# A hybrid decoder layer in five blocks: the edges between its stages rearranged, its up products cut into wider groups

## The chip, the cores and the metric

The kernel runs on one core of a Trainium2 chip. The metric is the device time of one execution in microseconds (us), median of three runs. The engines, as the profile names them: PE (TensorE, matmuls; PEld is its weight load), DVE (VectorE), ACT (ScalarE), POOL (GpSimd), SP (SyncE, which here only issues DMAs). Each engine runs its own instructions in order, and semaphores order them between engines. SBUF is the on-chip memory, PSUM the banks into which PE sums; DMAs move data between these and HBM.

## The reference

One decoder layer over 2048 prompt rows of 1024 columns and 8 x 4 sample rows. Norms are RMS norms; a conditioning vector gives a scale, a shift and a gate for each half of the layer.

```
mod  = silu(c) @ w_ada + b_ada                   # six vectors of 1024
h    = rmsnorm(x, g_pre_mix) * (1 + scale) + shift
p    = h @ w_in                                  # q, k, v, z, beta/decay; attention q, k, v
q, k, v = silu(causal conv, 4 taps)              # group A: gated DeltaNet, 4 heads x 128, chunked
oA   = gated delta rule(q, k, v, beta, g, state) # its state is an output, so is the conv's last rows
oB   = sliding window attention, window 128, with sinks   # group B: 8 query, 2 key heads x 64
x1   = x + gate * rmsnorm(concat(oA, oB) @ w_o, g_post_mix)
h2   = rmsnorm(x1, g_pre_ffn) * (1 + scale) + shift
y    = x1 + gate * rmsnorm(square(relu(h2 @ w_up)) @ w_down, g_post_ffn)   # 4096 hidden columns
```

Outputs are y for prompt and samples and the updated states and caches.

## The kernel before

All matrices are multiplied in three passes (`three_pass`, L79 to L84): both factors are split into a high and a low part of a reduced format, and hi x hi, hi x lo and lo x hi are summed in PSUM. ACT makes a high part by a casting copy, DVE the low part by subtracting it from the raw values. The layer is five blocks, one behind the other; at the end of each, its semaphores are cleared behind a barrier of all engines (`clear_sems`, L73), and the next block begins.

- `prologue` (L86): conditioning, the first four groups of w_ada (`group`, L286; `turn_rows` turns their rows into columns), small vectors turned into columns (L318 to L321), norm and turn of the first four x tiles and the samples (`square`, `norm`, `turn`, `evac`). SP issues every load; PE's turn of the vectors waits for all fifteen small loads, the last of which are the attention sinks (L139).
- `projection` (L339): h stays in SBUF, transposed, in four blocks of 512 rows plus 4 leading and 8 sample columns; w_in comes in 22 chunks of 128 columns for each block, 88 in all. For a chunk SP loads w_in (double buffered), ACT and DVE split it (`split`), PE sums two groups of 262 columns (48 matmuls), ACT evacuates (L568), and DVE and ACT run the four taps and silu (12 "conv" chunks of a block), silu alone, or a plain copy into `so`. POOL keeps the samples' columns and stores `so` to HBM (L793, through its software DMA queue); two zero stores (L778) begin its list. In the first three blocks, four x tiles each for the next block are squared, normed (`norm`, L700) and turned by PE (L463) between chunks: twelve in all.
- `mixer` (L1319): delta rule and attention tile by tile (16 tiles), an order written out by hand. POOL stores the outputs of a tile (L2178, L2182); at the end it waits for the last of them, issues four stores of states (L2207 to L2211), and waits for these.
- `out_projection` (L2228): tile by tile, 48 matmuls of 512 columns. At the start ACT and DVE split w_o (eight slices), PE spreads two gate rows (`spread_gate`, L2216), ACT evacuates them, and then the first tile's casts follow. `pre` is the product of a tile, `post` norm, gate and residual.
- `mlp` (L2499): two halves of the rows (`Half`, L2467; 1056 with the samples, 1024). Over pairs of hidden chunks, `up` makes 128 hidden columns at a time for all rows of the half, in four groups of 264 or 256 (one PSUM bank each), ACT relu, DVE square and split; `down` adds two hidden chunks' products to y for each tile of 128 rows (L2778). At a half's last `down`, each tile runs: add, mean square (ACT, DVE), pow -0.5 on POOL (L2737), scale and gate on DVE (`scale_out`, L2791), addition of x1 on POOL (`residual`, L2727), store by SP (L2603). POOL's order is pow of tile t, residual of tile t-1. SP loads x1 for tile t once tile t-2 is done. The second half's w_up and first up products stand behind or beside this.

Of the kernel before, what the change touches and what calls it, by code (L numbers as in the profile page):

```python
# [85 lines left out]
def prologue(nc, io, k):  # L86

    with ExitStack() as ctx:
# [17 lines left out]
        s_vec, s_c = m.sem("vectors_loaded"), m.sem("c_loaded")  # L106
# [9 lines left out]
        n_vec = 8 + 3 + NS  # L116
# [3 lines left out]
        with nc.Block() as block:  # L120
            @block.sync
            def _(sp):
                flat = lambda v: v.rearrange("a (c p) -> (a c) p", p=P)
                sp.dma_start(cin[0:1, :], io["c_prompt"]).then_inc(s_c, 16)
# [6 lines left out]
                for g in range(GA):  # L131
                    sp.dma_start(wa[:, g], io["w_ada"][:, g * 512:(g + 1) * 512].rearrange("(k p) n -> p k n", p=P)).then_inc(s_wa[g], 16)
                for t in ORDER:
                    src = io["xs"] if t == 4 else io["x"][t * P:(t + 1) * P, :]
                    sp.dma_start(xt[0:rows(t), t], src).then_inc(s_x[t], 16)
                for src, dst in ((io["a_log"], k["alog"]), (io["dt_bias"], k["dtb"]), (io["sinks"], k["sink"])):
                    sp.dma_start(dst[:], src.partition_broadcast(P).rearrange("p a h -> p (a h)")).then_inc(s_vec, 16)
                for s in range(NS):
                    sp.dma_start(k["sink_s"][s * 4:s * 4 + 4, :], io["sinks"].rearrange("a (g c) -> (a c) g", g=2), allow_slow_non_contiguous=True  # L139
                                 ).then_inc(s_vec, 16)  # L140
                sp.wait_ge(s_vec, 16 * n_vec)
# [41 lines left out]
            def _(act):  # L183
# [20 lines left out]
                square(0)  # L204
                square(1)
                for i in range(5):
                    if i + 2 < 5:
                        square(i + 2)
                    evac(i)

            @block.vector
            def _(dve):
# [11 lines left out]
                dve.wait_ge(s_tr, 2)  # L224
                v.tensor_copy(k["vcol"][:], pc[:, 0, 0:NV]).then_inc(s_der, 1)
                v.tensor_scalar(k["taps"][:], pc[:, 0, 96:96 + CW * CC], 0.5, None, ALU.mult).then_inc(s_der, 1)
                v.tensor_copy(k["xs_pad"][:, :, :, 0:CW - 1],
# [111 lines left out]
def projection(nc, io, k):  # L339
# [6 lines left out]
    with ExitStack() as ctx:  # L346
# [51 lines left out]
        with nc.Block() as block:  # L398
            @block.sync
            def _(sp):  # L400
# [25 lines left out]
                for b in range(NBLK):  # L426
                    for c in range(NCH):
                        n = b * NCH + c
                        if n + 2 < NBLK * NCH:
                            load(n + 2)  # L430
# [2453 lines left out]
```

## Time and profile before

| what | us |
|---|---|
| median of 3 runs (lowest, highest) | 2997.35 (2995.22, 2998.13) |
| the profiled execution | 2993.79 |
| its span | 2992.0 |
| PE busy / DVE / ACT / POOL | 2718.8 / 1475.2 / 866.8 / 293.5 |
| up products, L81 to L83, 2048 each line (the page's group means overlap) | 580.0 + 582.9 + 580.2 |
| DVE's adds of down products, L2778, 272 | 331.9 |
| POOL's chunk stores L793, 88 | 3.6 median to landing |

Times count from the start of the span. PE's matmuls are pipelined, so that the mean duration of one (283 ns for an up product) is longer than its spacing, and spacing is taken from stretches without gaps. "Idle before" is the time that an engine stood still before an instruction, with what released it. Lines of DMA issues (SPq, and on POOL) show the engine's issuing time, not the transfer; "to landing" runs from issue to the end of the transfer. Clearing and barriers at a block's end are no busy time and show as idle before the next block's first instructions, released by "PEq L76" or "POOLq L76".

### The profile page before, as it was taken

To read this page: it belongs to the slowest core of one execution; us is meant where nothing else is said; L and a number is where in the kernel's file an instruction comes from. 1 tells how busy PE (TensorE), PEld (TensorE's weight loads), DVE (VectorE), ACT (ScalarE), POOL (GpSimd) and SP (SyncE) were. 2 spreads that over 40 slices of the span, in tenths; PEclk is the share of its full clock that TensorE was granted. 3 is DMA by queue.
4 is the path that set the end of the run, shared out by engine and by line. 5 is a ranking of instruction groups with operands and counts; after the bars stand their busy time and mean duration, and the time that the engine had idled before them with its cause. 6 is when DMAs were issued, how large, how long until landed. Compare 5 with 4: busy or idle time off the path is not lost. (4 is left out here: it accounts for less than half of the span.)

```text
span 2992.0 us, 45904 instructions
## 1 busy us (share of the span) xinstructions
PE 2718.8 (91%) x18524; PEld 2390.3 (80%) x18524; DVE 1475.2 (49%) x2020; ACT 866.8 (29%) x1634; POOL 293.5 (10%) x417
## 2 busy tenths in 40 slices
PE   4999999996487896998799999999989999999996
PEld 2898999994265664886789989898968998998994
DVE  3646464636567774454444444434454434434434
ACT  2434343323054454332312112121222221221221
POOL 1111111111011111111000000000032000000004
PEclk7999999997698998999999999999999999999998
DMA  6554545345384455454311101010143111111113
GB/s 227 154 163 133 174 124 180 116 135 169 86 237 123 131 155 144 141 171 130 113 52 33 56 28 56 28 56 28 57 152 96 38 56 46 38 56 46 38 57 112
DMA packets 354361, 309.38 MB, mean 103 GB/s; under 512 B 41964, under 2 KB 308499, under 8 KB 354220
## 3 DMA queue, kind: packets, MB, share of 16 engines
q1 hardware_dynamic: 341196, 263.85, 30.2%
q0 software_dynamic: 13040, 43.81, 4.2%
q8 instruction: 86, 1.41, 0.2%
q14 instruction: 39, 0.32, 0.0%
HBM read 235.85 MB, written 72.70 MB: 103 GB/s over the span
## 5 line engine op out<-in xcount | busy, mean ns | idle before, releaser
L81 PE MATMUL up_ps<-h_hi,w_up_hi 128*128 128x264 f32 (+1 forms) x2048 | 580.0, 283 | 21.8 <-DVE h_lo L2756 15.6
L82 PE MATMUL up_ps<-h_lo,w_up_hi 128*128 128x264 f32 (+1 forms) x2048 | 582.9, 285 | 0.0
L83 PE MATMUL up_ps<-h_hi,w_up_lo 128*128 128x264 f32 (+1 forms) x2048 | 580.2, 283 | 0.0
L2778 DVE TENSOR_TENSOR y<-y,down_ps 128x1024 f32<-128x1024 f32 (+1 forms) x272 | 331.9, 1220 | 318.2 <-PE down_ps L83 317.7
L81 PE MATMUL down_ps<-w_down_hi,u_hi 128*128 128x512 f32 x1088 | 434.8, 400 | 18.4 <-issue 9.9
L83 PE MATMUL down_ps<-w_down_hi,u_lo 128*128 128x512 f32 x1088 | 430.4, 396 | 0.0
L82 PE MATMUL down_ps<-w_down_lo,u_hi 128*128 128x512 f32 x1088 | 428.5, 394 | 0.0
L81 PE MATMUL proj_ps<-h_hi,w_in_hi 128*128 128x262 f32 x1408 | 407.0, 289 | 14.8 <-DVE h_lo L656 11.6
L81 PEld LDWEIGHTS up_ps<-h_hi,w_up_hi 128*128 128x128 f32 x2048 | 388.9, 190 | 24.5 <-issue 16.9
L82 PE MATMUL proj_ps<-h_lo,w_in_hi 128*128 128x262 f32 x1408 | 402.1, 286 | 0.0
L83 PE MATMUL proj_ps<-h_hi,w_in_lo 128*128 128x262 f32 x1408 | 401.5, 285 | 0.0
L82 PEld LDWEIGHTS up_ps<-h_lo,w_up_hi 128*128 128x128 f32 x2048 | 388.2, 190 | 1.3
L83 PEld LDWEIGHTS up_ps<-h_hi,w_up_lo 128*128 128x128 f32 x2048 | 386.6, 189 | 0.0
L2768 DVE TENSOR_TENSOR relu<-relu 128x1056 f32<-128x1056 f32 (+1 forms) x64 | 81.6, 1274 | 492.3 <-ACT relu L2696 492.3
L81 PEld LDWEIGHTS proj_ps<-h_hi,w_in_hi 128*128 128x128 f32 x1408 | 267.8, 190 | 25.0 <-issue 24.6
L82 PEld LDWEIGHTS proj_ps<-h_lo,w_in_hi 128*128 128x128 f32 x1408 | 269.1, 191 | 0.0
L83 PEld LDWEIGHTS proj_ps<-h_hi,w_in_lo 128*128 128x128 f32 x1408 | 268.2, 190 | 0.0
L81 PEld LDWEIGHTS down_ps<-w_down_hi,u_hi 128*128 128x128 f32 x1088 | 206.1, 189 | 71.3 <-DVE y L2778 16.5
L83 PEld LDWEIGHTS down_ps<-w_down_hi,u_lo 128*128 128x128 f32 x1088 | 206.1, 189 | 48.5
L82 PEld LDWEIGHTS down_ps<-w_down_lo,u_hi 128*128 128x128 f32 x1088 | 207.2, 190 | 44.2
L2696 ACT ACTIVATE relu<-up_ps 128x264 f32<-128x264 f32 (+1 forms) x256 | 98.6, 388 | 486.3 <-PE up_ps L83 484.9
L2706 ACT CAST w_down_hi<-w_down_raw 128x1024 fp32r<-128x1024 f32 x64 | 64.0, 1049 | 603.4 <-PE down_ps L83 603.4
(494 smaller groups left out, 3667.4 us busy)
## 6 DMA issues: line engine op xcount, KB each, us to landing
w_in_raw<-in_w_in SPq DMA_DIRECT2D x88, 512.0 KB
w_up_raw<-in_w_up SPq DMA_DIRECT2D x66, 512.0 KB
w_down_raw<-in_w_down SPq DMA_DIRECT2D x64, 512.0 KB, 4.4
proj_scratch<-chunk_out POOLq DMA_DIRECT2D x88, 256.0 KB, 3.6
w_ada_cols<-in_w_ada SPq DMA_DIRECT2D x8, 2048.0 KB, 9.2
qkv<-proj_scratch SPq DMA_DIRECT2D x16, 768.0 KB, 6.8
p_w_ada_cols<-in_w_ada SPq DMA_DIRECT2D x4, 2048.0 KB, 15.3
prep_qk<-proj_scratch SPq DMA_DIRECT2D x16, 512.0 KB, 4.6
```

The costliest lines, as they stand in the source:

```text
L81: nc.tensor.matmul(out, whi, mhi, start=first, stop=False)
L82: nc.tensor.matmul(out, whi, mlo, start=False, stop=False)
L83: return nc.tensor.matmul(out, wlo, mhi, start=False, stop=last)
L2696: a.activation(ru[:, c, at], pu[:, j, 0:qn], ACT.Relu).then_inc(H.s_re, 1)
L2706: a.copy(dwh[:, c], dr[:, c]).then_inc(H.s_dwh, 1)
L2768: v.tensor_tensor(ru[:, c, 0:H.n], ru[:, c, 0:H.n], ru[:, c, 0:H.n], ALU.mult).then_inc(H.s_u, 1)
L2778: v.tensor_tensor(acc, acc, pd[r, (par * H.tiles + t) % 2], ALU.add).then_inc(H.s_y, 1)
```

## The change

In the order of the blocks. Prologue: loads in another order; the vectors' turn waits for eight loads, the other seven have a semaphore of their own; the norms and turns of x tiles lie between the groups; chunks 0 and 1 of w_in are loaded and split here. Projection: zero stores and chunk stores are issued by ACT; the store of chunk n-1 stands between the wait for chunk n's matmuls and chunk n's evacuation; one more `clear_sems` follows the block. Mixer: two state stores before the last tile's, two right behind the loop; their landing is waited for at the end of POOL's list in the out projection. Out projection: tile 0's casts before w_o's split, the first product waits slice by slice, the sample gate's spreading behind it. MLP: the second w_up load behind the h2 slices, h2 casts before its split and before the gate copies; groups of 352 columns (three) and 512 (two) instead of four; the residuals of odd tiles and of a half's last two tiles on DVE behind `scale_out`, with the semaphore of done tiles split by parity. The diff, cut:

```diff
                 sp.dma_start(cin[0:1, :], io["c_prompt"]).then_inc(s_c, 16)
                 sp.dma_start(cin[1:1 + NB, :], io["c_sample"]).then_inc(s_c, 16)
+                load_x(4)
+                load_ada(0)
+                load_x(0)
+                load_ada(1)
...
+                load_x(1)
+                load_ada(2)
+                load_x(2)
+                load_ada(3)
+                load_x(3)
+                for q in range(2):
+                    sp.dma_start(k["w_in_raw"][:, q], io["w_in"][:, q * P:(q + 1) * P].rearrange("(k p) n -> p k n", p=P)
+                                 ).then_inc(k["w_in_loaded"][q], 16)
...
+                                 ).then_inc(s_late, 16)
+                sp.wait_ge(s_late, 16 * (3 + NS))
...
-                square(0)
-                square(1)
-                for i in range(5):
-                    if i + 2 < 5:
-                        square(i + 2)
+                def split(n):
+                    act.wait_ge(k["w_in_loaded"][n], 16)
+                    a.copy(k["w_in_hi"][:, n], k["w_in_raw"][:, n]).then_inc(k["w_in_hi_split"], 1)
+
+                for i in range(4):
+                    square(i)
                     evac(i)
+                square(4)
+                split(0)
+                evac(4)
+                split(1)
...
+                norm(0)
                 rows_out(0)
+                norm(1)
                 rows_out(1)
+                dve.wait_ge(s_tr, 2)
...
                 columns(0)
+                norm(2)
+                columns(1)
                 rows_out(2)
-                columns(1)
-                norm(0)
-                norm(1)
+                norm(3)
+                columns(2)
                 rows_out(3)
-                columns(2)
-                norm(2)
+                norm(4)
                 columns(3)
...
+                turn(0)
                 group(0)
+                turn(1)
+                group(1)
                 pe.wait_ge(s_vec, 16 * n_vec)
...
                 last.then_inc(s_tr, 1)
-                group(1)
                 pe.wait_ge(s_der, 4)
                 turn_rows(0)
+                turn(2)
+                turn_rows(1)
                 group(2)
-                turn_rows(1)
+                turn(3)
+                turn_rows(2)
                 group(3)
-                turn_rows(2)
-                turn(0)
-                turn(1)
+                turn(4)
                 turn_rows(3)
...
-                load(0)
-                load(1)
+                load(2)
...
-                    if n >= 2:
-                        act.wait_ge(s_so, n - 1)
+                    if n > 0:
+                        store(n - 1)
                         act.wait_ge(s_keep, n - 1)
...
+                def store(n):
+                    c, at = n % NCH, n // NCH * BLK + PAD
+                    act.wait_ge(s_so, n + 1)
+                    act.dma_start(io["projT"][c:c + 1, :, at:at + BLK].rearrange("c p t -> (c p) t"), so[:, n % 2]).then_inc(s_st[n % 2], 16)
...
-                split(0)
-                split(1)
+                for q in range(2):
+                    act.dma_start(io["projT"][q * 11:q * 11 + 11, :, 0:PAD].rearrange("c p t -> p c t"),
+                                   k["zeros"][:].broadcast_to([P, 11, P])).then_inc(s_st[q], 16)
...
+                store(NBLK * NCH - 1)
+                for q in range(2):
+                    act.wait_ge(s_st[q], NBLK * NCH // 2 * 16 + 16)
...
-                    pool.wait_ge(s_so, n + 1)
-                    pool.dma_start(io["projT"][c:c + 1, :, b * BLK + PAD:(b + 1) * BLK + PAD].rearrange("c p t -> (c p) t"),
-                                   so[:, q]).then_inc(s_st[q], 16)
...
+                        if t == NT - 1:
+                            pool.wait_ge(s_st, NT)
+                            pool.dma_start(io["ssm_prompt"].rearrange("a b h k v -> k (a b h) v"), k["state"][:]).then_inc(s_fin, 16)
+                            pool.dma_start(io["swa_v_prompt"].rearrange("a b w g d -> (a b w) (g d)"), vt[:, 1, :]).then_inc(s_fin, 16)
...
-                pool.wait_ge(s_obst, 16 * NT)
-                pool.wait_ge(s_ost, 16 * NT)
-
-                pool.wait_ge(s_st, NT)
-                pool.dma_start(io["ssm_prompt"].rearrange("a b h k v -> k (a b h) v"), k["state"][:]).then_inc(s_fin, 16)
-                pool.dma_start(io["swa_v_prompt"].rearrange("a b w g d -> (a b w) (g d)"), vt[:, 1, :]).then_inc(s_fin, 16)
                 pool.wait_ge(s_fin0, 6)
                 pool.dma_start(io["swa_k_prompt"].rearrange("a b w g d -> (a b w) (g d)"), kl[:]).then_inc(s_fin, 16)
                 pool.dma_start(io["conv_prompt"].rearrange("a b i (c p) -> (a b i c) p", p=P), k["xrow"][:]).then_inc(s_fin, 16)
-                pool.wait_ge(s_fin, 64)
+                pool.wait_ge(s_obst, 16 * NT)
+                pool.wait_ge(s_ost, 16 * NT)
...
-                spread_gate(nc, pe, k, 0, TS, 0, True, pt[:, 1]).then_inc(s_gt, 1)

                 def pre(t, p, u):
-                    if isinstance(t, int) and t == 0:
-                        pe.wait_ge(s_wl, KD)
-                        pe.wait_ge(s_gr, 2)
                     pe.wait_ge(s_oh, t + 3)
                     pe.wait_ge(s_ol, t + 3)
                     pe.wait_ge(s_t, t + 1)
                     for kk in range(KD):
+                        if isinstance(t, int) and t == 0:
+                            pe.wait_ge(s_wl, kk + 1)
                         for h in range(2):
                             at = slice(h * 512, (h + 1) * 512)
                             last = three_pass(nc, po[:, p, h, :], ohi[:, p, kk, :], olo[:, p, kk, :],
                                               whi[:, kk, at], wlo[:, kk, at], kk == 0, kk == KD - 1)
                     last.then_inc(s_mm, 1)
+                    if isinstance(t, int) and t == 0:
+                        spread_gate(nc, pe, k, 0, TS, 0, True, pt[:, 1]).then_inc(s_gt, 1)

                 def post(t, p, u):
                     n = rows(t)
+                    pe.wait_ge(s_gr, 2)
...
+                act.wait_ge(s_w, 2 * KD * 16)
+                for c in range(KD):
+                    a.copy(whi[:, c], wr[:, c]).then_inc(s_wh, 1)
                 pre(1, 1, 0)
+                act.wait_ge(s_gt, 1)
+                a.copy(gate[:], pt[:, 0]).then_inc(s_gr, 1)
+                act.wait_ge(s_gt, 2)
+                a.copy(gate_s[:], pt[0:TS, 1]).then_inc(s_gr, 1)
...
+                pool.wait_ge(k["states_stored"], 64)
...
+        self.groups = 3 if half == 0 else 2
...
+    def on_dve(self, t):
+
+        return t % 2 == 1 or t == self.tiles - 1 or t == self.tiles - 2
...
-                for c in range(2):
-                    load_up(c, c, c)
+                load_up(0, 0, 0)
...
+                        load_up(1, 1, 1)
...
                 split_up(0, 0, 1)
+                h2_hi(first)
                 split_up(1, 1, 1)
                 act.wait_ge(s_gt, 1)
                 a.copy(gate[:], pd[:, 0]).then_inc(s_gr, 1)
                 act.wait_ge(s_gt, 2)
                 a.copy(gate_s[P - TS:P], pd[P - TS:P, 1]).then_inc(s_gr, 1)
-                h2_hi(first)
...
-                        if t > 0:
+                        if t > 0 and not H.on_dve(t - 1):
                             residual(t - 1)
-                    residual(H.tiles - 1)
...
+                        if H.on_dve(t):
+                            dve.wait_ge(H.s_yg, t + 1)
+                            dve.wait_ge(H.s_x[t % 2], 16 * (t // 2 + 1))
+                            if t % 2 == 0:
+                                dve.wait_ge(H.s_yo[0], t // 2)
+                            v.tensor_tensor(y[r, t], y[r, t], dr[r, t % 2], ALU.add).then_inc(H.s_yo[t % 2], 1)
...
+            early.clear_sems()
```

## Rows read from the trace of the kernel before

**Rows 1.** The page, first part: busy time, share of the span, instructions.
```profile
PE 2718.8 (91%) x18524; PEld 2390.3 (80%) x18524; DVE 1475.2 (49%) x2020; ACT 866.8 (29%) x1634; POOL 293.5 (10%) x417
```

**Rows 2.** Timeline of the opening: start, us, engine, line, tiles, count, idle before.
```profile
4.38 9.61 SPq L132 DMA_DIRECT2D p_w_ada_cols<-in_w_ada  x4
...
29.54 1.05 ACT L194 ACTIVATE p_x_squares<-p_x_tile 32x1024 f32<-32x1024 f32 x1 [25.27 <-DMA p_x_tile<-in_x_sample]
...
35.61 0.40 PE L318 MATMUL const_ps<-ident,vec_rows 81*128 81x81 f32 x1 [19.50 <-DMA sink_s<-in_sinks]
...
37.61 3.42 PE L292 MATMUL mod_ps<-p_w_ada_cols,scT 128*32 128x512 f32 x16
...
56.40 1.02 SPq L406 DMA_DIRECT2D w_in_raw<-in_w_in  x2
...
66.09 0.56 PE L81 MATMUL proj_ps<-h_hi,w_in_hi 128*128 128x262 f32 x1 [11.61 <-DVE h_lo L656]
```

**Rows 3.** Timeline of ACT, DVE and PE, one chunk with a norm.
```profile
242.54 0.61 ACT L568 ACTIVATE chunk_read<-proj_ps 128x524 f32<-128x524 f32 x1 [2.06 <-PE proj_ps L83]
...
247.09 0.68 DVE L691 SCALAR_TENSOR_TENSOR chunk_out<-chunk_out,chunk_convolved 128x512 f32<-128x512 f32 x1
...
249.94 1.09 PE L463 MATMUL side_ps<-ident,x_normed 128*128 128x128 f32 x8 [1.60 <-DVE x_normed L700]
```

**Rows 4.** Source view of L793, then of L2603: durations in ns.
```profile
L793 POOL DMA_DIRECT2D proj_scratch<-chunk_out x88: 539/539/950, 81.0 to 675.6; - x88
DMA to landing us min/median/max: 2.3/3.6/6.7
...
L2603 SPq DMA_DIRECT2D out_y_prompt<-y x16: 343/344/350, 2219.4 to 2988.2; - x16
```

**Rows 5.** Timeline of POOL at the projection's end.
```profile
675.59 0.54 POOL L793 DMA_DIRECT2D proj_scratch<-chunk_out  x1 [0.25 <-DVE chunk_out L687]
...
686.46 0.96 POOL L2160 MEMSET XT<- 128x1024 f32 x1 [10.34 <-POOLq L76]
```

**Rows 6.** Timeline of POOL at the mixer's end.
```profile
1179.40 0.75 POOL L2207 DMA_DIRECT2D out_ssm_prompt<-state  x1 [8.57 <-DMA mixed_scratch<-obT]
...
1181.22 0.55 POOL L2211 DMA_DIRECT2D out_conv_prompt<-xrow  x1
```

**Rows 7.** Timeline of the out projection's start, then a line of the DMA view.
```profile
1186.96 3.75 PE L2224 MATMUL turn_ps<-ident,gate_col 128*128 128x128 f32 x16 [18.21 <-PEq L76]
...
1187.98 9.17 DVE L2418 TENSOR_TENSOR w_o_lo<-w_o_raw,w_o_hi 128x1024 fp32r<-128x1024 f32 x8 [18.60 <-ACT w_o_hi L2362]
...
1198.85 0.77 PE L81 MATMUL out_ps<-w_o_hi,mixed_hi 128*128 128x512 f32 x1 [6.13 <-DVE mixed_lo L2425]
...
mixed_T<-mixed_scratch SPq DMA_DIRECT2D x16, 512.0 KB, 4.5
```

**Rows 8.** Timeline of the MLP's start.
```profile
1426.35 2.04 ACT L2677 CAST h_hi<-relu 128x1056 fp32r<-128x1056 f32 x2
```

**Rows 9.** Windows of steady up and down: PE, PEld, DVE, ACT, POOL busy, PEclk.
```profile
1560.89:1584.23 23.34, 23.34 (x194) 23.34 (x193) 7.24 (x6) 6.76 (x11) 0.00 (x0) 1.00 0.29 90
...
2309.69:2332.50 22.81, 22.81 (x193) 22.81 (x192) 7.08 (x6) 6.68 (x11) 0.00 (x0) 1.00 0.34 93
...
2332.50:2354.62 22.12, 22.12 (x98) 18.04 (x97) 12.03 (x10) 2.38 (x3) 0.00 (x0) 1.00 0.00 0
```

**Rows 10.** Source view of L2768 and L2727, timeline of the middle.
```profile
L2768 DVE TENSOR_TENSOR relu<-relu x64: 1219/1257/3296, 1453.1 to 2917.2; 128x1056 f32<-128x1056 f32 x32, 128x1024 f32<-128x1024 f32 x32
...
L2727 POOL TENSOR_TENSOR y<-y,w_down_raw x17: 2337/3417/3465, 2215.9 to 2985.9; 128x1024 f32<-128x1024 f32 x16, 32x1024 f32<-32x1024 f32 x1
...
2238.44 1.23 DVE L2778 TENSOR_TENSOR y<-y,down_ps 32x1024 f32<-32x1024 f32 x1
...
2246.98 3.30 DVE L2768 TENSOR_TENSOR relu<-relu 128x1024 f32<-128x1024 f32 x1
...
2249.42 3.11 POOL L2727 TENSOR_TENSOR y<-y,w_down_raw 32x1024 f32<-32x1024 f32 x1 [0.23 <-POOL y L2727]
```

More of the change, by code:

```diff
@@ L275, in _ @@
                 v.tensor_copy(k["pshift"][:, 0], k["modT"][:, 0:KD, 0]).then_inc(s_d, 1)
+                split(0)
+                split(1)
             @block.tensor
@@ L726, in _ @@
                 samples_lo(0)
-                split(0)
                 for kk in range(KD):
@@ L731, in _ @@
                         modulate(0, kk + 2)
-                split(1)
                 for b in range(NBLK):
@@ L776, in _ @@
                 g = nc.gpsimd
-                for q in range(2):
-                    pool.dma_start(io["projT"][q * 11:q * 11 + 11, :, 0:PAD].rearrange("c p t -> p c t"),
-                                   k["zeros"][:].broadcast_to([P, 11, P])).then_inc(s_st[q], 16)
                 def chunk(b, c):
@@ L2359, in _ @@
                     act.sem_inc(s, 2)
-                act.wait_ge(s_w, 2 * KD * 16)
-                for c in range(KD):
-                    a.copy(whi[:, c], wr[:, c]).then_inc(s_wh, 1)
-                act.wait_ge(s_gt, 1)
-                a.copy(gate[:], pt[:, 0]).then_inc(s_gr, 1)
-                act.wait_ge(s_gt, 2)
-                a.copy(gate_s[:], pt[0:TS, 1]).then_inc(s_gr, 1)
                 def pre(t, p, u):
@@ L2461, in _ @@
                 pre(0, 0, 0)
+                for c in range(KD):
+                    dve.wait_ge(s_wh, c + 1)
+                    v.tensor_tensor(wlo[:, c], wr[:, c], whi[:, c].bitcast(F32), ALU.subtract).then_inc(s_wl, 1)
                 pre(1, 1, 0)
+                dve.wait_ge(s_gr, 2)
                 skeleton(dve, lambda *_: None, post)
@@ L2474, in __init__ @@
         self.n = NT // 2 * P + (TS if half == 0 else 0)
-        self.last = 1 if half == 0 else 0
+        self.groups = 3 if half == 0 else 2
         self.ss, self.ms, self.rr = (m.sb(f"h{half}_{x}", [P, self.tiles]) for x in ("y_sumsq", "y_meansq", "y_rrms"))
@@ L2508, in mlp @@
         n0 = NT // 2 * P + TS
-        Q = 4
+        QM = 4
         NG = FF // P // 2
@@ L2579, in _ @@
                         h2_slices(H)
+                        load_up(1, 1, 1)
                     else:
-                        sp.wait_ge(first.s_yo, first.tiles)
+                        for q in range(2):
+                            sp.wait_ge(first.s_yo[q], first.count(q))
                     with sp.Fori(0, NG - 1) as G:
@@ L2838, in decoder_layer @@
         with ExitStack() as front:
-            for name, shape in (("xnT", [P, KD, LEAD + BLK]), ("xsT", [P, KD, TS]), ("modT", [P, 6 * KD, 9])):
+            for name, shape in (("xnT", [P, KD, LEAD + BLK]), ("xsT", [P, KD, TS]), ("modT", [P, 6 * KD, 9]), ("w_in_raw", [P, 2, KD, P])):
                 k[name] = Mem(nc, front).sb(name, shape)
+            for name in ("w_in_hi", "w_in_lo"):
+                k[name] = Mem(nc, front).sb(name, [P, 2, KD, P], FR)
+            early = Mem(nc, front)
+            k["w_in_loaded"] = [early.sem(f"w_in_loaded_{q}") for q in range(2)]
+            k["w_in_hi_split"], k["w_in_lo_split"] = early.sem("w_in_hi_split"), early.sem("w_in_lo_split")
             prologue(nc, io, k)
             projection(nc, io, k)
+            early.clear_sems()
         k["w_o_raw"] = m.sb("w_o_raw", [P, KD, D])
```

93 lines of the change are left out of this document (42 added, 51 removed).

## The prediction

> **What bounds the kernel now.** I read the page first: TensorE (PE) is busy for 2718.8 us, 91% of the span [rows 1], so some 270 us of idle PE plus the rate of its matmuls is all that can be won. The timeline then shows where PE stands still, because the change touches mostly those places: the opening, where PE waits 19.50 us for the last of fifteen small vector loads and starts its first projection matmul only at 66.09 [rows 2]; the end of the projection, where POOL begins the mixer 10.34 us after its last visible instruction [rows 5]; the end of the mixer, where it waits for the landing of the last tile before it issues four more stores [rows 6]; and the first matmul of the out projection at 1198.85 [rows 7]. Last, the windows view of steady stretches gives the rate of PE: it is busy without a gap, so there only fewer or cheaper matmuls help [rows 9].
>
> The profiled execution took 2993.79 us, 1.79 more than its span and 3.56 less than the median of the runs, 2997.35. I sum changes of the span and add 3.56 at the end, so the result stands against the median.
>
> **Opening: -14 (-17 to -11).** The pieces are in [rows 2]. Four weight loads of 2 MB are issued from 4.38, and the sample rows, queued behind them, have landed by 29.54: 8.1 MB in 25 us, some 5.5 us for each 2 MB, 1.3 for each 0.5 MB. In the new order the second weight group is there at about 19, the vectors at 20, the third at 27, the fourth at 34, the last x tile at 35, and the two early w_in chunks at 38. The transfers end no sooner; what goes is work that stood behind them. One group's matmuls take 3.42 on a PE that has idled [rows 2]; now three of the four lie beside the transfers, and with only the last still to do at 34, its rows, its columns, the last norm and turn, the derivations and two w_in_lo splits of about 1.2 follow one another until 46 to 50. I put the new block start at 50 against 56.40, and the first matmul 3.5 later (the zeros' two issues on ACT, sample cast, first slice) instead of 9.69, because w_in is split already: 53.5 against 66.09, -12.6, and about 1.3 more because chunk 1 then needn't wait for its weights. If turns and columns run at an idle PE's price too, and the late head vectors, issued last, land only behind w_in, the block starts at 52 (-11); if the last group runs at half its price, at 47 (-17).
>
> **Stores begun by ACT: +5 (+3 to +20).** POOL's 88 issues took 0.54 to 0.95 us each, beside everything else [rows 4]. ACT now waits for the next chunk's matmuls and for the preceding output, issues the store, and only then evacuates; queued behind that issue are the evacuation, DVE's convolution, and on twelve occasions the norm of an x tile, for whose turn PE waits. One such chain [rows 3]: evacuation 242.54, output 247.09, then the norm, and the turn at 249.94 after 1.60 us of PE idle for x_normed. There the issue delta lies on the path, 12 delta in all. In the other conv chunks of the first three blocks (24) and elsewhere, a chunk's ACT and DVE loop is some 5.27 us (242.54 to 247.09 + 0.68, and the hand-overs) against 48 matmuls at some 122 ns, 5.85, so delta is covered up to 0.58. No row shows ACT issuing a DMA. The nearest is SP's issue of a plain tile of 128 partitions, 0.34 [rows 4]; the far bound is POOL's 0.95. I take 0.4: 12 x 0.4 = +5. At 0.34 it is +4, with a bit of it hidden +3; at 0.95 it is 36 x 0.95 - 24 x 0.58 = +20. Nothing here can gain: POOL's issues were off the path.
>
> **End of the projection: -6.3 (-7 to 0).** The last store was issued at 675.59 and, by its group's shortest landing of 2.3 [rows 4], had landed at 677.9; yet the mixer starts at 686.46, 8.6 us after the landing [rows 5]. The mixer's own end, behind fewer stores of POOL, is shorter: its last store is issued at 1181.22, lands by 1183.5 if it takes 2.3 too, and the next block's PE starts at 1186.96, 3.4 later [rows 6, 7]. So the wait of 8.6 grows with POOL's DMAs, 90 here, and without any I expect 1 to 2 for the hand-over and 0.7 more for the extra clearing of semaphores: -6.3. If the 8.6 us have nothing to do with the stores, 0; if the hand-over is short, -7.
>
> **End of the mixer: -4 (-6 to -3).** POOL is idle for 8.57 us until 1179.40, when the last of oaT's and obT's stores has landed, and only then issues four more, the last from 1181.22 to 1181.77 [rows 6]; the next block starts 7.5 us after 1179.40 [rows 7]. New, the four go out before or just behind those two and are not waited for in this block (their wait lies at the end of the out projection). What goes is their issue, 2.4, and the rest of their landing, 1 to 2; what of the hand-over behind POOL's stores stays is the open part. The two moved ahead of oaT's store cost at most their 1.3 us of POOL, while the landing is set by queues that also carry w_o.
>
> **Out projection: -3 (-5 to -1).** The eight w_o_lo splits end at 1197.15, mixed_lo comes behind them, and the first matmul starts at 1198.85, 11.95 after the block's 1186.9 [rows 7]. New, tile 0's casts come first: mixed_T lands some 4.5 after its issue [rows 7], two casts 1.0 and 1.2, the first split 1.15 (9.17 / 8): PE starts at about 7.85, -4.1. After that it isn't held up: a slice's six matmuls take 1.38 at 230 ns [rows 9] against 1.15 of split. The sample gate's spreading moves behind the first tile and is on PE's path there: 16 matmuls, as the prompt gate's that take 3.75 on a PE just started [rows 7], but of a quarter of the stationary columns; between 0.5 and 2, I take 1.05.
>
> **MLP start: -0.5 (-2 to +1).** The first slice's cast at 1426.35 need not wait for the second w_up split and two gate copies [rows 8]: about -1.8. But w_up(1) is now issued behind all eight slices, and the two copies of 1.00 stand on ACT behind its split and before the first relu, which frees PE's first bank. The slices end at about the time that PE needs both; I let that take 1.3 back.
>
> **Up products: -17 (-22 to -14).** In steady stretches 192 matmuls of 264 columns take 23.34 us (121.6 ns each), 192 of 256 take 22.81 (118.8), and 96 down matmuls of 512 take 22.12 (230.4) (their counts hold two at the edges) [rows 9]. Half 2: two of 256 cost 237.6, one of 512 230.4, so 7.2 ns for each of 1536 removed, -11.1 us. Half 1: a line through 118.8 and 230.4 gives 160.6 ns for 352 columns; four of 264 against three of 352 is 486.4 - 481.8, times 768 sets -3.5; if a column costs 0.417 ns, an estimate of one cycle at the full granted clock of 1.00 (2.4 GHz), the 264 row leaves 11.6 ns a matmul, which makes 158.3 ns and -9. I take 160.0 (-5) and, for half 2, -12. PE is the bound in these stretches, DVE and ACT some 30% busy [rows 9], so the sum is not hidden. The Trainium skill ("TensorE: Matmul & The Clock Gate", section "Back-to-back issue gap") gives 2.5 ns over the columns for an isolated warm matmul; these rows show 12 to 17 ns.
>
> **Ends of the MLP halves: +1 and +0.5 (-3.3 and -2.7 to +2 each).** Today POOL sets the pace, 4.27 us a tile: pow 0.55 and residual 3.42 (the median of 17) [rows 10]. The same addition took 2.34 once, with DVE idle. And one DVE product of two SBUF inputs, 1.26 otherwise, took 3.30 from 2246.98, and ended at 2250.28, 1.09 after the residual that POOL ran until 2249.19 (0.23 ahead of its next) [rows 10]. So the two exclude one another, and only additions out of PSUM run beside POOL's. The moved residuals read two SBUF operands. Then a pair of tiles goes: add, mean square, pow, scale (1.28), POOL's residual of the even tile after that (2.34), DVE's residual of the odd one after that (1.25), and only then DVE's next add: 9.8 us a pair against 2 x 4.27 = 8.5. So the first half's last add comes 4.9 later than today. From it to the end of the last residual it is 14.1 us today (2238.44 to 2252.53 [rows 10]), with POOL two residuals behind; with the last two tiles on DVE I work out 10.4. That leaves +1.2, taken as +1; at the end of the kernel, a tile and a store less, +0.5. Without exclusion the residuals overlap, a pair takes about 7.6, the last add comes hardly later, and it is -3.3 and -2.7. A rule of the Trainium skill ("SBUF — State Buffer", section "SBUF: two separate sides") bears on it: DVE with two SBUF inputs and GpSimd take one shared port pair for a whole instruction and the other blocks. The trace agrees with that in the 3.30 us, and by it the moved residuals gain nothing.
>
> **Sum.** -14 + 5 - 6.3 - 4 - 3 - 0.5 - 17 + 1 + 0.5 = -38.3: profiled execution 2955.5, median of runs 2959.
>
> **Rivals.**
> - Residuals overlap (both ends gain): -38.3 - 4.3 - 3.2 = 2951. For it: POOL and DVE do overlap in the add; against it the 3.30 row. 0.17.
> - POOL's wait at the projection's end stays: +6.3, 2965. For it: I saw only that POOL came late, not why. 0.12.
> - A matmul's fixed cost is only 2.5 ns, as in that section of the skill: 2304 x 2.5 ns = -5.8 instead of -17, 2970. From the rows alone: a removed matmul must then save 2.5 ns instead of 5 to 8, which the 512 row contradicts. 0.08.
> - ACT's issues cost POOL's 0.95: +15, 2974. 0.14.
> - Slower: the issue on ACT, with its waits, decides. The rest is worth -43.3, and 36 delta - 14 exceeds that from delta = 1.6 us. At 2.0, +58, so 3012. For it: the new wait for the preceding output stands before each evacuation; against it, no issue of this shape took over 0.95 [rows 4]. 0.04.
> - The change doesn't do what it says in the opening: PE still waits for the transfers, -5 instead of -14, 2968. 0.08.
>
> **Numbers.** The forecast has 0.37. Those on the low side reach 2940 with the products' and opening's better ends; those on the high side reach 2974, and 2980 with a second small miss. Range 2938 to 2980. A measurement of this kernel can tell about 0.2%, 6 us, from no change: faster 0.93, same 0.03, slower 0.04.
>
> **What would show it.** First projection matmul near 53.5; ACT's issue near 0.4 us and PE's idle before the twelve turns longer by it; the mixer's first POOL instruction some 4 us after the last store's issue; 144 and 96 up matmuls in about 23.0 and 22.0 us; DVE residuals that last 2 to 3.6 us where POOL's runs beside them. Wrong would be: an ACT issue above 0.6, up matmuls at 160 ns and more for 352 columns with 235 for 512, a gap of 8 us or more before the mixer, or y adds at a steady 3 to 4 us.

## The result and the profile after

The changed kernel takes 2961.21 us (median of 4 runs, 2960.84 to 2966.52) against 2996.5 (4 runs, 2995.22 to 2998.13): ratio 0.9886, 95% interval 0.9874 to 0.9898. The forecast was 2959. Its profiled execution has a span of 2959.6, 32.4 less than before. Where these went, stage by stage between fixed points of the two traces (a matmul's start, unless said otherwise):

| stretch | before | after | difference | forecast |
|---|---|---|---|---|
| start to first projection matmul | 66.09 | 55.77 | -10.3 | -14 |
| first to last projection matmul | 607.81 | 612.70 | +4.9 | +5 |
| from there to the mixer's first POOL instruction | 12.56 | 5.38 | -7.2 | -6.3 |
| mixer, to the out projection's first matmul of the gate | 500.50 | 494.38 | -6.1 | -4 |
| out projection's start (11.89 to 7.77) and rest (217.34 to 219.31) | 229.23 | 227.08 | -2.1 | -3 |
| MLP to the first down matmul | 71.26 | 68.95 | -2.3 | -0.5, and products |
| first half and transition | 800.00 | 794.62 | -5.4 | |
| second half and end | 704.60 | 700.74 | -3.9 | |

The last two rows and part of the one above hold the up products (-17 forecast) and the ends of the halves (+1.5). The page of the changed kernel, its span, first part and DMA queues: ACT's stores have a queue of their own (q10), and POOL's busy time fell by 91 us.

```profile
span 2959.6 us, 41038 instructions
...
PE 2720.4 (92%) x16220; PEld 2314.7 (78%) x16220; DVE 1497.5 (51%) x2030; ACT 851.1 (29%) x1538; POOL 202.4 (7%) x317
...
q10 hardware_dynamic: 15520, 24.52, 2.3%
```

PE's busy time is what it was [rows 1] although 2304 matmuls are gone: by tile it is 16 us less in up products, 10 more in down products and 7 more in all others. So busy time does not tell what was won, and the table goes by fixed points.

The opening's timeline, columns as in [rows 2], and the windows view of it, where the value before the last two is the granted clock of PE:

```profile
28.86 3.64 PE L318 MATMUL mod_ps<-p_w_ada_cols,scT 128*32 128x512 f32 x16
...
32.57 0.69 DVE L248 COPY p_mod_rows<-mod_ps 128x512 f32<-128x512 f32 x1 [3.41 <-PE mod_ps L318]
...
33.98 0.75 DVE L262 TENSOR_SCALAR p_x_normed<-p_x_tile,p_x_rrms 128x1024 f32<-128x1024 f32 x1 [0.66 <-POOL p_x_rrms L195]
...
34.79 1.97 PE L338 MATMUL xT_ps<-ident,p_x_normed 128*128 128x128 f32 x8 [2.29 <-DVE p_x_normed L262]
...
38.20 3.64 PE L318 MATMUL mod_ps<-p_w_ada_cols,scT 128*32 128x512 f32 x16
...
55.77 0.56 PE L81 MATMUL proj_ps<-h_hi,w_in_hi 128*128 128x262 f32 x1 [8.16 <-DVE h_lo L688]
...
23.70:55.70 32.00, 17.58 (x80) 11.34 (x80) 11.01 (x30) 8.70 (x13) 1.65 (x3) 0.50 0.48 150
```

The two L318 rows are groups 2 and 3 of w_ada. Their weights had landed at 24.69 and 31.97, so they start 4 and 6 us late: DVE copies a group's rows, only then norms an x tile that has been there for some time, PE turns the tile and those rows, and only then does the next group start. Group 3 starts 9.34 us behind group 2. All of it ran at a granted clock of 0.50 (1.2 GHz).

ACT's stores in the source view, then one in ACT's timeline (at the chunk of [rows 3]): 0.33 us of issue, a little under the 0.34 of SP that was the low bound, and the evacuation behind it. The last three lines, from the tile view of x_normed for PE, are the sum of PE's idle time before the twelve turns of x tiles and their number, before (L700), after (L732) and in experiment 2 (L734).

```profile
L608 ACTq DMA_DIRECT2D proj_scratch<-chunk_out x88: 326/326/338, 71.3 to 670.3; - x88
DMA to landing us min/median/max: 2.0/2.0/7.2
...
233.02 0.33 ACTq L608 DMA_DIRECT2D proj_scratch<-chunk_out  x1
233.39 0.61 ACT L590 ACTIVATE chunk_read<-proj_ps 128x524 f32<-128x524 f32 x1 [2.41 <-PE proj_ps L83]
...
  DVE x_normed L700: 12.9, 12
...
  DVE x_normed L732: 16.8, 12
...
  DVE x_normed L734: 12.7, 12
```

The first POOL instruction of the mixer waits 3.57 us instead of 10.34 [rows 5], and the out projection's first matmul stands 7.8 us behind its block instead of 11.9 [rows 7]:

```profile
673.85 0.96 POOL L2181 MEMSET XT<- 128x1024 f32 x1 [3.57 <-POOLq L76]
...
1168.22 3.75 PE L2244 MATMUL turn_ps<-ident,gate_col 128*128 128x128 f32 x16 [12.83 <-PEq L76]
...
1175.99 0.77 PE L81 MATMUL out_ps<-w_o_hi,mixed_hi 128*128 128x512 f32 x1 [4.02 <-DVE w_o_lo L2481]
```

Windows of steady stretches, columns as in [rows 9]: second half up and down, first half up and down.

```profile
2281.32:2303.59 22.27, 22.27 (x98) 18.00 (x96) 7.08 (x6) 5.79 (x7) 0.00 (x0) 1.00 0.33 96
2303.59:2325.91 22.32, 22.32 (x98) 17.98 (x97) 12.02 (x10) 2.59 (x3) 0.00 (x0) 1.00 0.00 1
1537.54:1560.59 23.05, 23.05 (x145) 23.05 (x144) 7.24 (x6) 6.34 (x9) 0.00 (x0) 1.00 0.30 91
1560.59:1585.77 25.18, 25.18 (x110) 20.25 (x109) 13.43 (x11) 2.48 (x3) 0.00 (x0) 1.00 0.00 0
```

An up matmul of 352 columns takes 160.1 ns, one of 512 232.0. But the down products, which were not changed, went from 22.12 [rows 9] to 22.3 us a stretch. The start of such a stretch on DVE shows why: the last 512 columns of relu come late as one piece, and the three operations that follow fill DVE until the first addition, which comes 4.3 us after PE began the stretch, so PE waits 0.1 us for a bank at its third tile.

```profile
2304.42 1.22 DVE L2797 TENSOR_TENSOR relu<-relu 128x1024 f32<-128x1024 f32 x1 [7.50 <-ACT relu L2727]
...
2307.90 1.21 DVE L2807 TENSOR_TENSOR y<-y,down_ps 128x1024 f32<-128x1024 f32 x1
2309.36 1.22 DVE L2807 TENSOR_TENSOR y<-y,down_ps 128x1024 f32<-128x1024 f32 x1 [0.24 <-PE down_ps L83]
```

The end of the first half, timeline of POOL and DVE, and the source view of DVE's residual (L2826): while POOL's residual runs from 2188.72, DVE's takes 3.30 us, and the next add stands behind it. From add to add of a pair it is 9.63 us; 9.8 was worked out.

```profile
2188.72 3.43 POOL L2757 TENSOR_TENSOR y<-y,w_down_raw 128x1024 f32<-128x1024 f32 x1
...
2189.93 3.30 DVE L2826 TENSOR_TENSOR y<-y,w_down_raw 128x1024 f32<-128x1024 f32 x1
2193.15 1.21 DVE L2807 TENSOR_TENSOR y<-y,down_ps 128x1024 f32<-128x1024 f32 x1
...
L2826 DVE TENSOR_TENSOR y<-y,w_down_raw x10: 1222/2494/3301, 2189.9 to 2954.6; 128x1024 f32<-128x1024 f32 x9, 32x1024 f32<-32x1024 f32 x1
```

### The profile page after: what moved, and what is told of

Read it like the earlier page. It is cut to its first block and busy times, and to the rows that moved or that the text cites. A ratio compares the mean times of both kernels' runs of the same rounds, so it can differ in the third digit from the quotient of the medians.

```text
span 2959.6 us, 41038 instructions
## 1 busy us (share of the span) xinstructions
PE 2720.4 (92%) x16220; PEld 2314.7 (78%) x16220; DVE 1497.5 (51%) x2030; ACT 851.1 (29%) x1538; POOL 202.4 (7%) x317
## 5 line engine op out<-in xcount | busy, mean ns | idle before, releaser
L81 PE MATMUL up_ps<-h_hi,w_up_hi 128*128 128x352 f32 (+1 forms) x1280 | 449.6, 351 | 18.0 <-DVE h_lo L2785 13.6
L83 PE MATMUL up_ps<-h_hi,w_up_lo 128*128 128x352 f32 (+1 forms) x1280 | 449.3, 351 | 0.0
L82 PE MATMUL up_ps<-h_lo,w_up_hi 128*128 128x352 f32 (+1 forms) x1280 | 448.6, 350 | 0.0
L81 PEld LDWEIGHTS up_ps<-h_hi,w_up_hi 128*128 128x128 f32 x1280 | 240.1, 188 | 44.5 <-issue 18.1
L81 PEld LDWEIGHTS down_ps<-w_down_hi,u_hi 128*128 128x128 f32 x1088 | 207.8, 191 | 78.4 <-DVE y L2807 25.2
L82 PEld LDWEIGHTS up_ps<-h_lo,w_up_hi 128*128 128x128 f32 x1280 | 240.7, 188 | 23.3
L83 PEld LDWEIGHTS up_ps<-h_hi,w_up_lo 128*128 128x128 f32 x1280 | 240.5, 188 | 22.3
L2727 ACT ACTIVATE relu<-up_ps 128x352 f32<-128x352 f32 (+1 forms) x160 | 82.7, 519 | 487.7 <-PE up_ps L83 487.6
```

Source lines behind the costliest of these rows:

```text
L81: nc.tensor.matmul(out, whi, mhi, start=first, stop=False)
L82: nc.tensor.matmul(out, whi, mlo, start=False, stop=False)
L83: return nc.tensor.matmul(out, wlo, mhi, start=False, stop=last)
L2727: a.activation(ru[:, c, at], pu[:, j, 0:qn], ACT.Relu).then_inc(H.s_re, 1)
```

## Experiments

Times are medians of runs; the kernel before, run again beside each experiment, took 2996.9 to 2998.0, and the changed kernel, run again beside the last, 2959.83. Single executions of the changed kernel's code differ by some us in two stages where the code is the same: first to last projection matmul 608.3 to 614.5, mixer 493.5 to 498.5. So terms are read from their own stage.

**1. Stores by ACT alone, in the kernel before.**

```diff
+                    if n > 0:
+                        store(n - 1)               # ACT: wait s_so, issue; ahead of the evacuation
...
-                    pool.dma_start(io["projT"][c:c + 1, ...], so[:, q]).then_inc(s_st[q], 16)
```

> The kernel before with one part of the change: chunk stores and zero stores begun by ACT. Theory (the issue on ACT lies on the path of the twelve norms, and POOL's late end comes from its own stores): first to last projection matmul 4 to 5 us longer than before, the mixer's first POOL instruction 7 to 8 us nearer to the last projection matmul, together about 3 us faster than before. Rival (the wait before the mixer has nothing to do with POOL's stores): that gap stays at 12.5 us from the last matmul, the kernel 4 to 5 us slower than before.

2996.08 us, ratio to before 0.9996 (0.9987 to 1.0006): nothing. The two terms are there as the theory has them, projection 612.77 (+5.0), last projection matmul to mixer 4.99 instead of 12.56 (-7.6). What it left out is the opening, where the first matmul comes 3.0 later. The block begins 0.8 later, and ACT's casts of w_in at 62.11 and 65.14 instead of 60.26 and 62.17. ACT does not wait there for its own two issues of zero stores (1.57 us, over at 58.75) but for the loads of w_in. The zero stores, begun by ACT, move beside these loads from 59 on; POOL's, in the kernel before, moved nothing until 61. That this traffic slows the loads fits the times but was not tested by itself. In the changed kernel both chunks are loaded ahead of the block. ACT's wait, and the mixer's start:

```profile
62.11 1.04 ACT L552 CAST w_in_hi<-w_in_raw 128x1024 fp32r<-128x1024 f32 x1 [5.81 <-DMA w_in_raw<-in_w_in]
...
686.81 0.96 POOL L2163 MEMSET XT<- 128x1024 f32 x1 [3.18 <-POOLq L76]
```

**2. The store behind the evacuation.**

```diff
-                    if n > 0:
-                        store(n - 1)
+                    if n > 1:
+                        act.wait_ge(s_so, n - 1)
                         act.wait_ge(s_keep, n - 1)
                     a.mul(xb[:, q, :] ...).then_inc(s_ev, 1)
+                    if n > 0:
+                        store(n - 1)
```

> The changed kernel, with ACT's store of a chunk placed behind the next chunk's evacuation instead of ahead of it. Theory (the 0.4 us of issue ahead of the evacuation is what the projection lost): first to last projection matmul back to the 607.8 us of before, 4 to 5 us faster than the changed kernel. Rival (ACT's wait for the preceding output, or the stores' traffic, costs it): the projection stays at 612.7 us, no difference.

2955.36 us, 4 to 6 faster than the changed kernel; projection 603.90. Against the eight executions of the changed kernel's code with the store ahead (mean 611.6) that is -7.8, against the shortest -4.4. The steady part is plain in PE's idle time before the twelve turns, shown above: 12.9 us before, 16.8 with the store ahead (16.7 in the second execution), 12.7 here. So the issue costs 4 us; the first turn waits no longer (0.27 in both), the other eleven 0.33 to 0.41 each, and six of the chunks that hold such a turn take 8.80 to 8.85 us instead of 8.43. The rest are single chunks that come and go and take 1 us or so more; why they are fewer here is open.

**3. Four groups again.**

```diff
-        self.groups = 3 if half == 0 else 2
+        self.groups = 4
```

> The changed kernel with four groups of 264 and 256 columns in the up products, as before. Theory (a removed matmul saves some 5 to 8 ns, and the wider last group makes DVE reach its first add later, which costs the down products 0.1 to 0.2 us a stretch): up stretches 23.34 and 22.81 us, down stretches back to 25.11 and 22.12, the kernel 9 to 10 us slower than the changed one. Rival (the down products became slower for another reason, such as a denser PE): down stretches stay at 25.18 and 22.31, the kernel 13 us slower.

2970.15 us, 9 to 10 slower than the changed kernel. The down stretch is back at 22.12 with the narrow groups, so the wide group causes its 0.2 us. Windows of one up and one down stretch of the second half:

```profile
2336.76:2359.57 22.81, 22.81 (x194) 22.81 (x192) 7.08 (x6) 6.68 (x11) 0.00 (x0) 1.00 0.30 92
2359.57:2381.69 22.12, 22.12 (x98) 18.03 (x97) 12.03 (x10) 2.38 (x3) 0.00 (x0) 1.00 0.00 0
```

**4. The opening in another order.**

```diff
                 norm(0)
-                rows_out(0)
                 norm(1)
+                rows_out(0)
                 rows_out(1)
...
+                norm(2); columns(0); columns(1); norm(3); rows_out(2); columns(2); norm(4)
+                rows_out(3); split(0); split(1); columns(3)           # DVE
...
+                turn(2)                                               # PE, ahead of turn_rows(0), (1)
```

> The changed kernel with the opening's order changed once more: DVE's norm of an x tile ahead of the copy of the next group's rows, PE's turns ahead of the row turns, both w_in splits ahead of the last columns. Theory (the opening ended 2 us later than forecast because in-order DVE chains norm, turn, row turn and group, not because of transfers): first projection matmul at 45 to 48 instead of 55.8, 8 to 10 us faster than the changed kernel. Rival (transfers and the clock of an idle PE bound it): first matmul within 2 us of 55.8.

ACT's second split of w_in moves ahead of its last evacuation too. 2953.18 us, 7 to 8 faster than the changed kernel. Group 2 starts at 27.76, group 3 at 33.45, 1.0 behind the landing of its weights, and the first projection matmul at 45.26, 10.5 earlier with the same loads in the same order; the rival is out. But the order is not all of it: from 32 to 39 PE was granted the clock of 1.00 here, and its five pieces behind group 2 (turn, row turn, group 3, turn, row turn) took 6.3 us instead of 11.0 (group 3 alone 1.92 instead of 3.64). So up to 4.7 of the 10.5 us came with the clock, which rose under the new order; what part that order would gain at 0.50 was not measured.

```profile
27.76 3.64 PE L318 MATMUL mod_ps<-p_w_ada_cols,scT 128*32 128x512 f32 x16
...
33.45 1.92 PE L318 MATMUL mod_ps<-p_w_ada_cols,scT 128*32 128x512 f32 x16
...
32.10:38.70 6.60, 5.16 (x46) 3.54 (x44) 3.29 (x7) 4.73 (x6) 0.55 (x1) 1.00 0.63 151
...
45.26 0.56 PE L81 MATMUL proj_ps<-h_hi,w_in_hi 128*128 128x262 f32 x1 [6.74 <-DVE h_lo L688]
```

**5. Every residual on DVE.**

```diff
     def on_dve(self, t):
-        return t % 2 == 1 or t == self.tiles - 1 or t == self.tiles - 2
+        return True
```

> The changed kernel with every residual on DVE, none on POOL. Theory (DVE's and POOL's residuals exclude one another, which stretches DVE's from 1.25 to 2.5 or 3.3 us): all residuals of 128 rows 1.25 us, a pair of tiles 8.8 us instead of 9.6, a half's last residual 3 us sooner after its first add (42 to 43 us instead of 45.9 in the first half), kernel 3 to 6 us faster than the changed one. Rival (DVE's residual is slow by itself or by the loads of x1): residuals still above 2 us, a pair longer than 9.6 us, kernel slower.

2955.51 us, 4 to 6 faster than the changed kernel. All seventeen take 1.23 us, in the source view; a pair 8.80, last residual of the first half 41.7 after the first add, end of the kernel 40.8 instead of 44.7.

```profile
L2822 DVE TENSOR_TENSOR y<-y,w_down_raw x17: 1223/1225/1227, 2190.7 to 2950.5; 128x1024 f32<-128x1024 f32 x16, 32x1024 f32<-32x1024 f32 x1
```

**6. Every residual on POOL.**

```diff
-        return t % 2 == 1 or t == self.tiles - 1 or t == self.tiles - 2
+        return False
...
+                    residual(H.tiles - 1)                             # POOL
```

> The changed kernel with every residual on POOL, as before the change. Theory (the moved residuals gain nothing at the pair, 9.6 against 8.5 us, and little at the end): first half's last add 4 to 5 us earlier than in the changed kernel, its last residual 44.9 us after its first add instead of 45.9, end of the kernel 0.5 to 1 us earlier after the last half's first add; kernel within 3 us of the changed one. Rival (moving them to DVE gained the 3 us at each end that they cost on POOL): 5 to 6 us slower than the changed kernel.

2963.21 us, 2 to 3 above the changed kernel's two medians, which is too little to tell from no difference. Last add 4.4 earlier, last residual 44.9, end 44.2: as expected. Yet the second half's first down product comes 80.9 us after the first add, against 78.4 in the changed kernel (80.6 in its second execution). PE ran out of work at 2228 and stood until 2235, and until 2241 the granted clock was 0.50 (1.2 GHz). In the changed kernel it stood 2.5 us there and the clock was 1.00; in that kernel's second execution it stood 4.0 us, the clock was 0.50, and the second half's first pair of up products, the stop included, took 51.3 instead of 47.6. The length of a stop does not decide this by itself: at the first half's last tiles the changed kernel's PE stood 2.63 and 2.25 us, and after each the clock was 0.50 for 3.4 us. Below are PE's rows at a stop and windows behind it (the seventh value after the range is the clock): of this kernel, of the changed one, of its second execution, and at the two stops of the changed kernel's last tiles:

```profile
2234.84 0.80 PE L81 MATMUL up_ps<-h_hi,w_up_hi 128*128 128x512 f32 x1 [6.65 <-ACT relu L2727]
...
2234.50:2239.50 5.00, 4.66 (x11) 3.70 (x12) 5.00 (x6) 4.30 (x6) 0.00 (x0) 0.50 0.01 3
```
```profile
2236.20:2240.00 3.80, 3.51 (x15) 2.90 (x16) 3.80 (x5) 3.10 (x5) 0.00 (x0) 1.00 0.00 0
...
2236.49 0.51 PE L81 MATMUL up_ps<-h_hi,w_up_hi 128*128 128x512 f32 x1 [2.47 <-ACT relu L2727]
```
```profile
2232.00:2237.00 5.00, 4.11 (x10) 3.24 (x11) 5.00 (x5) 4.30 (x7) 0.28 (x1) 0.50 0.01 3
...
2232.89 0.80 PE L81 MATMUL up_ps<-h_hi,w_up_hi 128*128 128x512 f32 x1 [3.98 <-ACT relu L2727]
```
```profile
2194.42 0.74 PE L81 MATMUL down_ps<-w_down_hi,u_hi 128*128 128x512 f32 x1 [2.63 <-DVE y L2807]
...
2204.05 0.50 PE L81 MATMUL down_ps<-w_down_hi,u_hi 128*128 128x512 f32 x1 [2.25 <-DVE y L2807]
...
2194.50:2197.90 3.40, 3.40 (x8) 2.68 (x9) 2.48 (x3) 1.41 (x3) 0.80 (x2) 0.50 0.89 286
2204.70:2208.10 3.40, 3.40 (x10) 2.62 (x9) 2.72 (x4) 1.41 (x3) 0.69 (x2) 0.51 0.91 341
```

**7. Every residual on DVE, between mean square and scale of the next tile.**

```diff
                         v.tensor_scalar(H.ms[r, t:t + 1], ...).then_inc(H.s_ms, 1)
...
+                        if t > 0:
+                            residual(t - 1)
                         dve.wait_ge(H.s_rr, t + 1)
```

> The changed kernel with every residual on DVE, each placed between the mean square and the scale of the next tile, where DVE otherwise waits 0.66 us for POOL's power. Theory: residuals 1.25 us, a pair 7.4 to 7.6 us, the first half's last residual 37 to 39 us after its first add instead of 45.9, the end 5 to 7 us sooner after the last half's first add; kernel 10 to 13 us faster than the changed one. Rival (the transition is set by the second half's weights and the x1 loads): a pair 7.5 us too, but the first down product of the second half comes no sooner, and the gain is the end's 5 us alone.

2948.9 us, 11 to 12 faster than the changed kernel. Residuals 1.22; a pair 8.1, not 7.5, because POOL's power, beside a DVE residual, takes 1.46 us instead of 0.55 (the first of the two POOL lines, with no residual beside it), and DVE's scale waits for it. Last residual 39.05 after the first add, end 38.8 instead of 44.7, and the first down product of the second half comes 6.6 sooner after the first add: the rival is out.

```profile
2179.57 0.55 POOL L2765 TENSOR_TENSOR h_y_rrms<-h_y_meansq,nhalf 128x1 f32<-128x1 f32 x1 [782.67 <-DVE h_y_meansq L2814]
...
2182.56 1.21 DVE L2826 TENSOR_TENSOR y<-y,w_down_raw 128x1024 f32<-128x1024 f32 x1
...
2182.72 1.46 POOL L2765 TENSOR_TENSOR h_y_rrms<-h_y_meansq,nhalf 128x1 f32<-128x1 f32 x1 [2.59 <-DVE h_y_meansq L2814]
```

**8. The MLP's start.**

```diff
+                            if H is first and kk == 4:
+                                load_up(1, 1, 1)                      # SP, among the slices
...
+                        if H is first and kk == 2:                    # ACT, likewise the second at 4
+                            a.copy(gate[:], pd[:, 0]).then_inc(s_gr, 1)
```

> The changed kernel with the second w_up chunk issued ahead of the fifth h2 slice's sample piece and the two gate copies between h2 casts (behind the third and the fifth). Theory (in the changed kernel the second chunk's split and the gate copies stand between the last slice and the first relu): 1.5 to 2 us less from the first up to the first down matmul (59.8 us now). Rival (the slices are paced by their loads, and a w_up load among them delays them by as much): 59 to 61 us, no gain.

2963.55 us, first up to first down 59.8: no gain, as the rival has it. The slices are cast as their loads land, and from the fifth on, behind the w_up load, the casts came 1.4 to 2.1 us later after the first up matmul than in the changed kernel.

**9, 10. Edits 2, 4 and 7 together, and the changed kernel again.**

> The changed kernel with the three edits that the runs so far bear out: stores behind the evacuation, the opening's second order, and every residual on DVE between mean square and scale. Theory (the three act in different stages and add): first projection matmul at 45.3, projection 604 to 608 us, end of the first half's residuals 39 us after its first add, 24 to 31 us faster than the changed kernel, 2930 to 2938. Rival (part of a stage's gain is given back at the next wait, as with the mixer's loads): less than 20 us faster, above 2941.

> The changed kernel unaltered, as the measure for the run before on the same chip: 2961 us within 5.

2934.12 us (5 runs), ratio to before 0.9784 (0.9768 to 0.9799), against 2959.83 for the changed kernel on the same chip: 25.7 faster. First matmul 46.37, projection 603.89, the first half's last residual 39.07 after its first add. Alone the three edits gave 4 to 6, 7 to 8 and 11 to 12: they add up.

## Why the prediction was right

The forecast of the median was 2 us low, 2959 against 2961.21. That is closer than its parts deserve. The profiled execution was forecast at 2955.5 and took 2961.36, as the sum came to -32.4 and not -38.3; the 3.56 us added for the median, which the kernel after did not show, made up for most of that. And within the sum, the opening and the up products gave 11 us less than forecast, while the end of the projection, the mixer, the MLP's start and its transition gave 6 to 7 more, 4 of which are no more than single executions differ by. So the size of the total is in part luck. That the kernel became faster, and by which stages, is not; the single steps:

- **Opening**, -14 forecast, -10.3 measured, outside its range. The block start was put at 50 and came at 52.1. The step that failed is "with only the last still to do at 34": three of the four groups did lie beside the transfers, but the last one, whose weights were there at 31.97, started at 38.20, behind the in-order chain of DVE and PE. The price named for the low end, turns and columns at an idle PE's price and the block at 52, is what came: the granted clock was 0.50 from 23.7 to 55.7. Experiment 4 took 10.5 us out of chain and clock together with the same transfers. The further 1.3 for chunk 1 did not come either: the first chunk's period is 9.37 in both traces. The landing of 5.5 us for each 2 MB does not follow from 8.1 MB in 25 us, which is 6.2; with an x tile of 0.5 MB between them the groups landed 7.0 to 7.6 apart, and still the third and fourth were there 2 us before the 27 and 34 that were assumed.
- **Stores on ACT**, +5 and +4.9. The mechanism is the one described: PE's wait before the twelve turns grew by 3.9 us, eleven delays and not twelve, and experiment 2 takes them away. The other 1.0 is within what this stage varies. The slower rival needed 1.6 us for an issue; it is 0.33.
- **End of the projection**, -6.3 and -7.2; experiment 1 shows it alone. The rival that POOL's late end stays is out.
- **End of the mixer**, -4 and -6.1. From the landing of the last obT store to the next block's PE it is 3.9 us instead of 8.3 (1164.32 to 1168.22; before 1178.69 to 1186.96), so -4.4. The further 1.7 lies within what the mixer varies. No run has this edit alone.
- **Out projection**, -3 and -2.1: the first matmul came 4.1 sooner as worked out; the rest lost 2.0 instead of 1.05, most of it in the first tile, 15.18 us to the second instead of 13.68, where the spreading of the sample gate takes PE 1.94. No run has this edit alone.
- **MLP start**, -0.5 and -1.7 (the -2.3 less two narrower up stretches of 0.29): the first up matmul came 3.5 sooner instead of 1.8, and 1.8 was given back behind it instead of 1.3.
- **Up products**, -17 forecast, some -9.6, outside its range: the term that was mis-sized most. The half with 352 columns is right (160.1 ns, 16 stretches by -0.29, -4.7). At 512 columns the down products' 230.4 ns was taken, and 0.9 us more without a row for it; it is 232.0, so 16 by -0.54, -8.6. And the down products gave back 15 by 0.18 and 15 by 0.07, 3.7 us, which "the sum is not hidden" overlooked: PE was the bound, but DVE's first add was not far behind it. A removed matmul saved 6.0 ns in the first half's up stretches and 5.6 in the second's, so the rival at 2.5 ns is out. In the Trainium skill ("TensorE: Matmul & The Clock Gate", "Back-to-back issue gap") the 2.5 ns over the columns is the gap of an isolated matmul. It is not that of these dense stretches, where 512 columns stand 18.7 ns over 512 / 2.4.
- **Ends of the halves**, +1 and +0.5. From the first add to the last residual of the first half it was 44.9 us before and is 45.8, and from the last half's first add to the end 43.8 and 44.7: +0.9 each. The exclusion of DVE's and POOL's additions with two SBUF inputs carried this: DVE's residual takes 1.23 us with POOL silent (experiment 5) and 2.4 to 3.3 beside POOL's, and in experiment 7 it is POOL's power that is held up. The Trainium skill ("SBUF — State Buffer", "SBUF: two separate sides") states such a lock, and these runs agree. The whole transition, the products' share taken out, came out at -1.3 in this execution and +0.9 in the second one of the same kernel, where PE's stop before the second half's first up products was 4.0 us and not 2.5 and the clock behind it 0.50. Why the stop differs is open.

## What to carry to other kernels

An operation moved to another engine to share work is worth nothing if the two engines exclude one another at it: look in the trace for an operation that took twice its median, and what ran beside it. Here all of it on one engine, in a gap where that engine waited anyway, gained 11 to 12 us, where sharing gained nothing that the runs could tell. Fewer and wider matmuls gained some 6 ns here for each that went, and one must look at what the wider last piece delays behind it. When an opening is fed by loads, write each engine's order by the time at which its input lands; an item placed behind a wait that it doesn't need holds everything that follows. Last, a sum that meets its forecast shows nothing about its terms: compare stage by stage, and run one kernel twice to see how far a stage varies.

## What the runs showed of the hardware

- A DMA issued by ACT costs it 0.33 us for 128 rows of 2 KB, POOL 0.54 to 0.95; the first lands in 2.0 us at the median, the second in 3.6.
- POOL's power of 128 values takes 0.55 us alone and 1.46 when a DVE addition of two SBUF operands, begun just before it, runs beside it; DVE's addition takes 1.22 us alone and 2.4 to 3.3 beside POOL's. So each holds up the other.
- After PE's stops of 4.0 and 6.65 us the granted clock was 0.50 for 4.8 and 6.2 us. After stops of 2.63 and 2.25 us in one trace it was 0.50 for 3.4 us, and after one of 2.47 us in the same trace it was 1.00. So a stop under 3 us can cost the clock, and its length alone does not tell.
- Fp32r matmuls (the reduced format) of 256, 264, 352 and 512 columns in dense streams stand 118.8, 121.6, 160.1 and 230.4 to 232.0 ns apart at a granted clock of 1.00.
